# Gathered expert rows in a decoder layer: weighted rows in batches of two, tables asked for in turn

## The chip, the cores and the metric

The kernel runs on one core of a Trainium2 chip. The metric is the device time of one execution in microseconds (us); less is better.

## What is computed

One layer of a decoder over 1024 prompt tokens and 32 sample tokens (8 sequences of 4), width 1024, fp32: modulated RMSNorm, an input projection, a short gated convolution beside windowed attention, an output projection, and then a layer of 16384 single-neuron experts. This last part takes most of the time:

```
q = (x @ wq).reshape(tokens, 8 heads, 2, 128)
sc = einsum('thpc,hpnc->thpn', q, keys)            # 128 keys for each half
s_top, i_top = top_k(sc, 16)
best, pos = top_k(sum of all 16 x 16 pairs, 16)
experts = i_top[0] * 128 + i_top[1] at pos
act = gelu(einsum('thkd,td->thk', u_tab[experts], x))
y = einsum('thk,thkd->td', softmax(best) * act, v_tab[experts])
```

So each token needs, for 8 heads, 16 rows of `u_tab` and 16 of `v_tab`, each 1024 floats (4 KB). The outputs are the normed sums and the new key, value and convolution states.

## The kernel before, in words

**Units.** The tokens stand in 33 groups of 32. A unit is one group with four heads: 128 partitions (32 tokens x 4 heads), 16 experts each, so 66 units (`UNITS`). For a unit the kernel gathers 16 U rows and 16 V rows; one gather brings one row for each of 128 partitions, 128 x 4 KB, by an indirect DMA of GpSimd. Both tables have a ring of eight rows in SBUF, `Ur` and `Vr` (`RING` = 8).

**GpSimd** (`gather_u`, line 510, gather at 516; `gather_v`, gather at 527) asks for the rows in program order. U rows go in batches of two, each of which waits until DVE has done the dots of the batch four before (`dots_done`); batch 0 of a unit waits for its indices (`idx_ready`). V rows go in batches of four (`VB` = 4, four batches a unit, `NV`, over two ring halves), each of which waits until PE has weighed the batch two before (`pv_done`). The order is two U batches of unit n, one V batch of unit n-1, and so on. At the end, V rows of the last unit go to the U ring (`gather_last`, 536) and to the V ring (558).

**DVE** does the dots (`dots`, 1557: one instruction a row, 1024 products against the replicated token, summed), and between the batches of unit n the six parts of the top-16 selection of unit n+1 (`top`, 1505 to 1551; the last writes the indices `eid` at 1551, after the dots of batch 5), and pieces of earlier stages. **ACT** does gelu (1160), the softmax exponent (1123), and builds 16 diagonal blocks `dsel` of 128 x 32 that hold the weights (`selectors`, 1168).

**PE** sums the weighted rows: `weigh(m, q)` multiplies `dsel` (32 columns) with V rows 4q to 4q+3, first the four rows on columns 0 to 511 into bank 0, then on columns 512 to 1023 into bank 1; row k writes the 32 partitions `j = k % 4`. Each matmul shows as two instructions in the trace. Two units (the two halves of the heads) add up in the banks:

```
for half in range(2):
    for k in range(q * VB, (q + 1) * VB):
        j = k % 4
        last = mm(PS[j * GT:(j + 1) * GT, half, :], dsel[m % 2][:, k, :], rows[:, k % RING, half * 512:(half + 1) * 512], ...)
```

Then ACT copies both banks to `Yp` (`take_y`, 1178), and `combine` (862) sums the four blocks of 32 partitions through `sel` (four identity blocks below each other). `gated` and `normed` on DVE finish 128 tokens at a time.

**Order around it.** PE, ACT and DVE each run a loop over units n with four slots q. In a slot PE does the first piece of `gap(n, q)`, the combine (slot 1 of odd n), the other pieces, queries or scores for later tokens, and at its end `weigh(n-1, q)`. `replicate` (764), which puts the group's tokens where DVE reads them, stands ahead of slot 0 of even n. The pieces are what is left of the earlier stages, in a fixed list (`WOVEN`) dealt out by rules of load (`gaps`, at most 1, 3, 2 and 1 in slots 0 to 3): X transposes (660), Q and W query and score products (667, 676), I input projection (684), VN, KN, UT transposes (601, 603, 656), S, P, V of attention (618, 624, 629), H0, H1 output projection (696), T transposes (701). A piece on PE waits for the copy of the one before it by ACT or DVE; pieces go up to unit 20. Of its slots 17 hold more than one, for example:

| unit | slot 0 | slot 1 | slot 2 | slot 3 |
|---|---|---|---|---|
| 1 | T | X, X, X | X, X | Q |
| 3 | Q | Q | Q, W | W |
| 13 | I | I, VN, KN | UT, S | S |
| 14 | P | S, P, V | S, P | S |
| 18 | H1 | T, H0 | H1, T | H0 |

Of the kernel before, what the change touches and what calls it, by code (L numbers as in the profile page):

```python
# [7 lines left out]
D = 1024  # L8
# [27 lines left out]
VB = 4  # L36
# [88 lines left out]
def build(nc, a, out):  # L125
    ctx = ExitStack()
    with ctx:
# [80 lines left out]
        Yp, x2b, g2v, gfv = (R(38048 + D * i, D) for i in range(4))  # L208
# [238 lines left out]
        def _(po):  # L447
# [84 lines left out]
            def gather_last(q):  # L532

                po.wait_ge(s["dots_done"], (UNITS - 1) * NU + 6 + 2 * q)
                for k in range(q * VB, (q + 1) * VB):
                    po.indirect_dma_start(
                        out=Ur[:, k % RING, :], out_offset=None, in_=a["peer_v"],
                        in_offset=bass.IndirectOffsetOnAxis(ap=eid[(UNITS - 1) % 4][:, k:k + 1], axis=0),
                    ).then_inc(last_ld[q], 16)

            for n in range(UNITS - 1):
                for q in range(NV):
                    if n < UNITS:
                        gather_u(n, 2 * q)
                        gather_u(n, 2 * q + 1)
                    if n >= 1:
                        gather_v(n - 1, q)
            for q in range(NV):
                gather_u(UNITS - 1, 2 * q)
                gather_u(UNITS - 1, 2 * q + 1)  # L550
                if q == NV - 1:
                    gather_last(0)
                gather_v(UNITS - 2, q)
            gather_last(1)
            for q in (2, 3):
                po.wait_ge(s["pv_done"], (UNITS - 2) * NV + q + 1)
                for k in range(q * VB, (q + 1) * VB):
# [3 lines left out]
                    ).then_inc(v_ld[q % VBUFS], 16)  # L561
# [3 lines left out]
        def _(pe):  # L565
# [271 lines left out]
            def weigh(m, q):  # L837
                pe.wait_ge(s["diag_ready"], m + 1)
                rows = Vr
                if m < UNITS - 1:  # L840
                    pe.wait_ge(v_ld[q % VBUFS], 16 * VB * ((m * NV + q) // VBUFS + 1))
                elif q < 2:
                    pe.wait_ge(last_ld[q], 16 * VB)
                    rows = Ur
                else:
                    pe.wait_ge(v_ld[q % VBUFS], 16 * VB * (m * NV // VBUFS + 1))
                if q == 0 and m % 2 == 0 and m >= 2:
                    pe.wait_ge(s["y_ev"], m // 2)
                for half in range(2):
                    for k in range(q * VB, (q + 1) * VB):  # L850
                        j = k % 4
                        last = mm(PS[j * GT:(j + 1) * GT, half, :], dsel[m % 2][:, k, :], rows[:, k % RING, half * 512:(half + 1) * 512],  # L852
                                  start=m % 2 == 0 and q == 0, stop=m % 2 == 1 and q == NV - 1)
                last.then_inc(s["pv_done"], 1)

            def combine(g):
# [4 lines left out]
                for half in range(2):  # L861
                    last = mm(PS[p:p + GT, 2 + half, :], sel[:, :], Yp[:, half * 512:(half + 1) * 512], start=True, stop=True)  # L862
# [5 lines left out]
            for n in range(UNITS + 2):  # L868
# [3 lines left out]
                for q in range(NV):  # L872
# [8 lines left out]
                    if q == NV - 1 and FIRST <= n + 2 < UNITS:  # L881
                        scores(n + 2)
                    if q == NV - 1 and n == FIRST - 1 or q == 1 and n >= FIRST and t < TT:
                        queries(t, h)
                    if 1 <= n <= UNITS:
                        weigh(n - 1, q)
# [3 lines left out]
        def _(ac):  # L890
# [280 lines left out]
            def take_y(g):  # L1171
                ac.wait_ge(s["pv_done"], min(2 * g + 2, UNITS) * NV)
                if g:
                    ac.wait_ge(s["pe_cmb"], g)
                if g == 0:
                    ac.wait_ge(s["sc_st"], 16)
                for half in range(2):
                    last = act_(Yp[:, half * 512:(half + 1) * 512], PS[:, half, :], ACT.Copy)  # L1178
                last.then_inc(s["y_ev"], 1)

            for n in range(UNITS + 2):
# [8 lines left out]
                left = gap(n - 1, NV - 1)  # L1190
# [12 lines left out]
                for q in range(NV - 1):  # L1203
# [473 lines left out]
```

## Time and profile before

| | us |
|---|---|
| median of 3 timed executions | 3490.13 |
| lowest, highest | 3469.93, 3493.14 |
| profiled execution, span from first to last instruction | 3228.3 |

The profile shows one execution, and of its time only the span; start and end of the program lie around it. In its rows PE is TensorE, PEld its weight load, DVE VectorE, ACT ScalarE, POOL GpSimd, SP the sync engine; "L852" is a line of the kernel. The idle time before an instruction is put down to what ended it; "issue" means that no wait ended it. [...]

### The profile page before, as it was taken

To read this page: it belongs to the slowest core of one execution; us is meant where nothing else is said; L and a number is where in the kernel's file an instruction comes from. 1 tells how busy PE (TensorE), PEld (TensorE's weight loads), DVE (VectorE), ACT (ScalarE), POOL (GpSimd) and SP (SyncE) were. 2 spreads that over 40 slices of the span, in tenths; PEclk is the share of its full clock that TensorE was granted. 3 is DMA by queue.
4 is the path that set the end of the run, shared out by engine and by line. 5 is a ranking of instruction groups with operands and counts; after the bars stand their busy time and mean duration, and the time that the engine had idled before them with its cause. 6 is when DMAs were issued, how large, how long until landed. Compare 5 with 4: busy or idle time off the path is not lost.

```text
span 3228.3 us, 31544 instructions
## 1 busy us (share of the span) xinstructions
PE 1830.4 (57%) x9976; PEld 857.1 (27%) x9976; DVE 2038.7 (63%) x5142; ACT 705.5 (22%) x1970; POOL 2058.7 (64%) x2211
## 2 busy tenths in 40 slices
PE   5998757776746776374444444444444444454543
PEld 2456543333312222141111212211121112121200
DVE  3335736666668867566666766666666666666663
ACT  2122112212214322122222211122222222211211
POOL 1233647676656656577777777777777777777774
PEclk8999778888867787686676666677767767666567
DMA  9727999999999999999999999999999999999997
GB/s 325 262 96 247 366 395 385 410 410 410 410 342 367 378 372 409 406 409 410 409 407 405 402 411 405 407 402 410 402 407 404 406 406 405 403 408 402 406 408 298
DMA packets 393188, 1228.50 MB, mean 381 GB/s; under 512 B 54563, under 2 KB 104719, under 8 KB 389678
## 3 DMA queue, kind: packets, MB, share of 16 engines
q0 software_dynamic: 305728, 1109.92, 86.8%
q1 hardware_dynamic: 46314, 75.12, 6.6%
q10 hardware_dynamic: 40980, 41.44, 3.9%
q8 instruction: 79, 1.29, 0.2%
q14 instruction: 87, 0.71, 0.1%
HBM read 1211.31 MB, written 16.04 MB: 380 GB/s over the span
## 4 chain that ended last, share of the span: by engine, by line
POOL 30%; DMA 28%; DVE 15%; issue 12%; PE 11%; DVEq 2%; ACTq 1%; ACT 1%; SPq 1%; POOLq 0%
DMA arena<-in_peer_u,eid 22%; POOL arena L516 15%; POOL arena L527 14%; DVE arena L1557 9%; DMA arena<-in_peer_v,eid 4%; PE PS L722 3%; PE PS L852 2%; PE PS L696 1%; DVE arena L1546 1%; ACTq L956 1%; PE PS L684 1%; PE PS L667 1%; DVE ef L1549 1%; DVE arena L1541 1%; PE PS L580 1%
## 5 line engine op out<-in xcount | busy, mean ns | idle before, releaser
L1557 DVE CUSTOM_DVE_ANT_0 arena<-arena,PS 128x1024 f32<-128x1024 f32 x1056 | 1244.3, 1216 | 795.9 <-DMA arena<-in_peer_u,eid 606.7
L852 PE MATMUL PS<-arena 128*32 128x512 f32 x4224 | 829.8, 924 | 1162.5 <-DMA arena<-in_peer_v,eid 1145.4
L516 POOL DMA_INDIRECT arena<-in_peer_u,eid x1056 | 997.8, 945 | 491.7 <-issue 294.7
L527 POOL DMA_INDIRECT arena<-in_peer_v,eid x1040 | 982.8, 945 | 476.3 <-issue 290.5
L852 PEld LDWEIGHTS PS<-arena 128*32 128x32 f32 x4224 | 165.8, 144 | 1611.4 <-issue 1604.3
L1168 ACT ACTIVATE arena<-sel,wgt 128x32 f32<-128x32 f32 x1056 | 230.7, 310 | 21.5 <-DVE wgt L1568 21.0
L684 PE MATMUL PS<-arena 128*128 128x256 f32 (+1 forms) x576 | 176.9, 463 | 14.3 <-DVE arena L1400 14.3
L822 PEld LDWEIGHTS PS<-arena 128*128 128x128 f32 x1280 | 156.3, 203 | 48.0 <-issue 48.0
L822 PE MATMUL PS<-arena 128*128 128x128 f32 x1280 | 163.7, 289 | 0.0
L1156 ACT ACTIVATE arena<-PS 128x256 f32<-128x256 f32 x42 | 16.1, 384 | 661.3 <-PE PS L833 661.3
L1151 ACT ACTIVATE arena<-PS 128x256 f32<-128x256 f32 (+1 forms) x48 | 17.1, 357 | 612.6 <-PE PS L822 612.6
L684 PEld LDWEIGHTS PS<-arena 128*128 128x128 f32 x576 | 114.7, 205 | 99.7 <-issue 40.7
L722 PE MATMUL PS<-arena 128*128 128x416 f32 x288 | 115.4, 547 | 6.5 <-DMA arena<-in_w_in 4.6
L696 PE MATMUL PS<-arena 128*128 128x512 f32 (+1 forms) x192 | 88.8, 617 | 9.1 <-ACT arena L1051 9.1
L1557 DVE DVE_READ_ACCUMULATOR2_ANT act<- 128x1 f32 x1056 | 87.0, 82 | 0.0
L1160 ACT ACT_TABLE_LOAD x66 | 84.7, 1283 | 1.2
L1123 ACT ACT_TABLE_LOAD x62 | 79.5, 1283 | 2.7 <-ACT arena L1051 1.2
L862 PE MATMUL PS<-arena,sel 128*32 128x512 f32 x132 | 74.3, 691 | 1.2 <-ACT arena L1178 1.2
L1178 ACT ACTIVATE arena<-PS 128x512 f32<-128x512 f32 x66 | 35.8, 594 | 172.9 <-PE PS L852 172.9
L722 PEld LDWEIGHTS PS<-arena 128*128 128x128 f32 x288 | 54.9, 200 | 58.7 <-issue 52.5
L1568 DVE SCALAR_TENSOR_TENSOR wgt<-gex,grec,gel 128x16 f32<-128x16 f32 x66 | 15.6, 236 | 75.0 <-ACT gel L1160 74.4
L667 PEld LDWEIGHTS PS<-arena 128*128 128x128 f32 x512 | 59.1, 196 | 7.9 <-issue 6.5
(241 smaller groups left out, 1958.0 us busy)
## 6 DMA issues: line engine op xcount, KB each, us to landing
arena<-in_w_ada SPq DMA_DIRECT2D x24, 1024.0 KB, 8.3
arena<-in_peer_u,eid POOLq DMA_INDIRECT x1056
arena<-in_peer_v,eid POOLq DMA_INDIRECT x1056, 7.1
arena<-in_peer_wq ACTq DMA_DIRECT2D x10, 1024.0 KB, 5.6
arena<-in_peer_wq SPq DMA_DIRECT2D x4, 2048.0 KB, 37.9
arena<-in_w_in SPq DMA_DIRECT2D x14, 512.0 KB, 8.1
arena<-in_w_in ACTq DMA_DIRECT2D x14, 512.0 KB, 15.0
arena<-in_x_prompt ACTq DMA_DIRECT2D x8, 512.0 KB, 8.4
```

The costliest lines, as they stand in the source:

```text
L516: po.indirect_dma_start(out=Ur[:, k % RING, :], out_offset=None, in_=a["peer_u"], in_offset=bass.IndirectOffsetOnAxis(ap=eid[m % 4][:, k:k ...
L527: po.indirect_dma_start(out=Vr[:, k % RING, :], out_offset=None, in_=a["peer_v"], in_offset=bass.IndirectOffsetOnAxis(ap=eid[m % 4][:, k:k ...
L667: last = mm(PS[:, 6 + n % 2, half * 256 + (t - 1) * 128:half * 256 + t * 128], wqA[(PH - 3 + n) % 3][:, k, half * 128:(half + 1) * 128], ( ...
L684: last = mm(PS[:, 6 + half, 0:hi - lo], winB[pos % 3][:, k, :], hTB[:, k, lo:hi], start=k == 0, stop=k == KT - 1)
L696: last = mm(PS[0:r, 6 + half, :], zq[n][:, k, :], wout[:, k, half * 512:(half + 1) * 512], start=k == 0, stop=k == KT - 1)
L722: last = mm(PS[:, pos % 4, 0:NA], win[pos % 4][:, k, :], hT[:, k, :], start=k == 0, stop=k == KT - 1)
L822: last = mm(PS[:, 6, half * r:(half + 1) * r], wq[:, k, c * 128:(c + 1) * 128], rhs[:, k, :], start=k == 0, stop=k == KT - 1)
L852: last = mm(PS[j * GT:(j + 1) * GT, half, :], dsel[m % 2][:, k, :], rows[:, k % RING, half * 512:(half + 1) * 512], start=m % 2 == 0 and q ...
L1123: act_(gex[:, par, :], best[:, par, :], ACT.Exp, bias=nbest[:, par, :], accum_out=gsum[:, par:par + 1]).then_inc(s["exp_done"], 1)
L1160: act_(gel[:, m % 2, :], act[:, m % 2, :], ACT.Gelu).then_inc(s["gelu_done"], 1)
L1168: last = act_(dsel[par][:, k, :], sel[:, :], ACT.Copy, scale=wgt[:, par, k:k + 1])
L1557: last = ve.tensor_tensor_reduce(out=Ur[:, k % RING, :], in0=Ur[:, k % RING, :], in1=hP, scale=1.0, scalar=0.0, op0=ALU.mult, op1=ALU.add, ...
```

## The change

V rows go in batches of two as well: eight batches a unit over four ring parts. GpSimd asks for two U rows and two V rows in turn. `weigh` takes two rows on both column halves: row k, half h writes the 32 partitions `2h + k % 2` of one bank, and the bank changes with every pair of units, so that `take_y` is one instruction and may lag by one pair. `Yp` becomes two buffers of 512 columns, and `combine` contracts 64 partitions for each half. PE weighs the first batch of a slot behind the slot's first piece, ahead of the combine and the other pieces, and the second at the slot's end.

```diff
-VB = 4
+VB = 2
...
-        Yp, x2b, g2v, gfv = (R(38048 + D * i, D) for i in range(4))
+        Yp = [R(38048 + 512 * i, 512) for i in range(2)]
+        x2b, g2v, gfv = (R(39072 + D * i, D) for i in range(3))
...
             for n in range(UNITS - 1):
-                for q in range(NV):
-                    if n < UNITS:
-                        gather_u(n, 2 * q)
-                        gather_u(n, 2 * q + 1)
+                for b in range(NV):
+                    gather_u(n, b)
                     if n >= 1:
-                        gather_v(n - 1, q)
+                        gather_v(n - 1, b)
...
-            def weigh(m, q):
+            def weigh(m, b):
...
-                if q == 0 and m % 2 == 0 and m >= 2:
-                    pe.wait_ge(s["y_ev"], m // 2)
-                for half in range(2):
-                    for k in range(q * VB, (q + 1) * VB):
-                        j = k % 4
-                        last = mm(PS[j * GT:(j + 1) * GT, half, :], dsel[m % 2][:, k, :], rows[:, k % RING, half * 512:(half + 1) * 512],
-                                  start=m % 2 == 0 and q == 0, stop=m % 2 == 1 and q == NV - 1)
+                if b == 0 and m % 2 == 0 and m >= 4:
+                    pe.wait_ge(s["y_ev"], m // 2 - 1)
+                for k in range(b * VB, (b + 1) * VB):
+                    for half in range(2):
+                        j = 2 * half + k % 2
+                        last = mm(PS[j * GT:(j + 1) * GT, m // 2 % 2, :], dsel[m % 2][:, k, :], rows[:, k % RING, half * 512:(half + 1) * 512],
+                                  start=m % 2 == 0 and b == 0, stop=m % 2 == 1 and b == NV - 1)
...
-                    last = mm(PS[p:p + GT, 2 + half, :], sel[:, :], Yp[:, half * 512:(half + 1) * 512], start=True, stop=True)
+                    last = mm(PS[p:p + GT, 2 + half, :], sel[half * 64:half * 64 + 64, :], Yp[g % 2][half * 64:half * 64 + 64, :], start=True, stop=True)
...
-                for q in range(NV):
+                for q in range(4):
                     for i in gap(n, q)[:1]:
                         piece(i)
+                    if 1 <= n <= UNITS:
+                        weigh(n - 1, 2 * q)
                     if q == 1 and n % 2 == 1 and n >= 3:
                         combine((n - 3) // 2)
...
                     if 1 <= n <= UNITS:
-                        weigh(n - 1, q)
+                        weigh(n - 1, 2 * q + 1)
...
-                if g:
-                    ac.wait_ge(s["pe_cmb"], g)
+                if g >= 2:
+                    ac.wait_ge(s["pe_cmb"], g - 1)
...
-                for half in range(2):
-                    last = act_(Yp[:, half * 512:(half + 1) * 512], PS[:, half, :], ACT.Copy)
-                last.then_inc(s["y_ev"], 1)
+                act_(Yp[g % 2], PS[:, g % 2, :], ACT.Copy).then_inc(s["y_ev"], 1)
```

GpSimd where unit 1 ends and unit 2 begins, before (`eid` with a number is the unit's index buffer, u and v the tables):

```order
L527 DMA arena<-in_peer_v,eid0 128x1024 x4
L516 DMA arena<-in_peer_u,eid1 128x1024 x4
L527 DMA arena<-in_peer_v,eid0 128x1024 x4
L516 DMA arena<-in_peer_u,eid2 128x1024 x4
L527 DMA arena<-in_peer_v,eid1 128x1024 x4
```

and the same place in the changed kernel (line 517 is the U gather, 528 the V gather):

```order
L517 DMA arena<-in_peer_u,eid1 128x1024 x2
L528 DMA arena<-in_peer_v,eid0 128x1024 x2
L517 DMA arena<-in_peer_u,eid1 128x1024 x2
L528 DMA arena<-in_peer_v,eid0 128x1024 x2
L517 DMA arena<-in_peer_u,eid2 128x1024 x2
L528 DMA arena<-in_peer_v,eid1 128x1024 x2
```

Batch 5 of U is the first half of the four U rows in the second line of the first piece, and the first line of the second piece is batch 6.

PE in unit 14, from `replicate` on, before (852 weighs, 764 replicates, 624 is P, 618 S, 629 V of attention):

```order
L764 MATMUL PS<-ident,arena 128x128 x8
L624 MATMUL PS<-ident,arena 128x128 x8
L852 MATMUL PS<-arena 32x512 x8
L618 MATMUL PS<-arena 128x256 x4
L624 MATMUL PS<-ident,arena 128x128 x8
L629 MATMUL PS<-arena 64x512 x4
L852 MATMUL PS<-arena 32x512 x8
L618 MATMUL PS<-arena 128x256 x4
L624 MATMUL PS<-ident,arena 128x128 x8
L852 MATMUL PS<-arena 32x512 x8
```

and in the changed kernel (851 weighs, the pieces' lines are two less):

```order
L762 MATMUL PS<-ident,arena 128x128 x8
L622 MATMUL PS<-ident,arena 128x128 x8
L851 MATMUL PS<-arena 32x512 x8
L616 MATMUL PS<-arena 128x256 x4
L851 MATMUL PS<-arena 32x512 x4
L622 MATMUL PS<-ident,arena 128x128 x8
L627 MATMUL PS<-arena 64x512 x4
L851 MATMUL PS<-arena 32x512 x4
L616 MATMUL PS<-arena 128x256 x4
L851 MATMUL PS<-arena 32x512 x4
L622 MATMUL PS<-ident,arena 128x128 x8
L851 MATMUL PS<-arena 32x512 x4
```

In slots with one piece the two batches stay side by side (x8). In slots 1 and 2 the first stands between the S piece and the P piece.

## Rows read from the trace of the kernel before

**Rows 1.** The page's parts 1 and 2: busy times, DMA share and GB/s in 40 slices.
```profile
PE 1830.4 (57%) x9976; PEld 857.1 (27%) x9976; DVE 2038.7 (63%) x5142; ACT 705.5 (22%) x1970; POOL 2058.7 (64%) x2211
...
DMA  9727999999999999999999999999999999999997
GB/s 325 262 96 247 366 395 385 410 410 410 410 342 367 378 372 409 406 409 410 409 407 405 402 411 405 407 402 410 402 407 404 406 406 405 403 408 402 406 408 298
```

**Rows 2.** Windows of two stretches: time, busy times of engines, PEclk, DMA share, GB/s.
```profile
600.00:800.00 200.00, 140.13 (x592) 69.60 (x593) 130.69 (x329) 45.46 (x126) 134.88 (x141) 0.85 1.04 410
2000.00:2200.00 200.00, 92.78 (x560) 38.29 (x562) 133.88 (x347) 43.69 (x125) 144.76 (x155) 0.69 1.02 405
```

**Rows 3.** Waits of GpSimd, 1400 to 3100 us: total, times, longest.
```profile
POOL arena L516 <- DVE eid L1551: 81.4, 41, 2.8
POOL arena L527 <- PE PS L852: 20.1, 25, 2.8
```

**Rows 4.** Timeline 2007 to 2030 us: start, length, engine, line, [idle before <- releaser].
```profile
2007.10 1.22 DVE L1557 CUSTOM_DVE_ANT_0 arena<-arena,PS 128x1024 f32<-128x1024 f32 x1
...
2011.05 0.18 DVE L1551 SCALAR_TENSOR_TENSOR eid<-ef 128x16 int32<-128x16 f32 x1
...
2011.49 0.94 POOL L516 DMA_INDIRECT arena<-in_peer_u,eid  x1 [2.29 <-DVE eid L1551]
...
2012.73 0.94 POOL L516 DMA_INDIRECT arena<-in_peer_u,eid  x1 [0.30 <-issue]
...
2021.36 3.64 PE L852 MATMUL PS<-arena 128*32 128x512 f32 x16 [5.70 <-DMA arena<-in_peer_v,eid]
```

**Rows 5.** Windows of the seven stalls of the DMA queue, columns as in rows 2.
```profile
346.00:362.00 16.00, 9.04 (x44) 5.00 (x48) 13.78 (x38) 1.68 (x3) 5.87 (x7) 0.61 0.59 203
478.00:496.00 18.00, 11.76 (x232) 8.29 (x232) 8.62 (x28) 10.55 (x25) 7.23 (x8) 0.83 0.79 238
910.00:926.00 16.00, 10.04 (x53) 4.28 (x53) 14.66 (x31) 2.23 (x5) 5.81 (x7) 0.79 0.60 198
976.00:990.00 14.00, 10.58 (x57) 4.48 (x54) 11.79 (x23) 5.29 (x15) 7.36 (x8) 0.87 0.75 261
1022.00:1034.00 12.00, 8.00 (x44) 3.70 (x40) 10.12 (x20) 4.00 (x16) 7.45 (x8) 0.80 0.85 293
1066.00:1080.00 14.00, 10.80 (x56) 4.50 (x56) 11.20 (x22) 3.73 (x12) 6.09 (x6) 0.81 0.68 236
1170.00:1188.00 18.00, 15.38 (x55) 6.14 (x57) 4.16 (x5) 1.44 (x3) 7.50 (x8) 0.97 0.73 261
```

**Rows 6.** Timeline of PE and GpSimd in the stall at 980 us.
```profile
959.00 1.99 PE L618 MATMUL PS<-arena 64*128 64x256 f32 x8
...
968.89 1.97 PE L624 MATMUL PS<-ident,arena 128*128 128x128 f32 x8 [7.90 <-DVE arena L1417]
...
977.55 2.64 PE L852 MATMUL PS<-arena 128*32 128x512 f32 x16
...
980.51 0.94 POOL L527 DMA_INDIRECT arena<-in_peer_v,eid  x1 [11.00 <-PE PS L852]
```

**Rows 7.** First request after the stall at 915 us, and the queue two us later.
```profile
918.36 0.95 POOL L527 DMA_INDIRECT arena<-in_peer_v,eid  x1 [12.81 <-PE PS L852]
...
920.00:922.00 2.00, 2.00 (x12) 1.35 (x15) 2.00 (x5) 0.00 (x0) 1.49 (x2) 1.00 0.91 245
```

**Rows 8.** Waits of DVE, 940 to 1100 us: the first.
```profile
DVE arena L1557 <- DMA arena<-in_peer_u,eid: 20.2, 6, 15.2
```

**Rows 9.** Timeline of PE in the stall at 480 us.
```profile
481.30 3.32 PE L676 MATMUL PS<-arena 128*32 128x128 f32 x64 [26.78 <-ACT arena L1033]
```

**Rows 10.** The chain that ended last, at the end.
```profile
3213.07 1.96 PE PS L852 x16
3215.05 1.09 ACT arena L1178 x2
3216.19 1.92 PE PS L862 x4
```

More of the change, by code:

```diff
@@ L534, in gather_last @@
                 po.wait_ge(s["dots_done"], (UNITS - 1) * NU + 6 + 2 * q)
-                for k in range(q * VB, (q + 1) * VB):
+                for k in range(q * RING // 2, (q + 1) * RING // 2):
                     po.indirect_dma_start(
@@ L541, in _ @@
             for n in range(UNITS - 1):
-                for q in range(NV):
-                    if n < UNITS:
-                        gather_u(n, 2 * q)
-                        gather_u(n, 2 * q + 1)
+                for b in range(NV):
+                    gather_u(n, b)
                     if n >= 1:
-                        gather_v(n - 1, q)
-            for q in range(NV):
-                gather_u(UNITS - 1, 2 * q)
-                gather_u(UNITS - 1, 2 * q + 1)
-                if q == NV - 1:
+                        gather_v(n - 1, b)
+            for b in range(NV):
+                gather_u(UNITS - 1, b)
+                if b == NV - 1:
                     gather_last(0)
-                gather_v(UNITS - 2, q)
+                gather_v(UNITS - 2, b)
             gather_last(1)
-            for q in (2, 3):
-                po.wait_ge(s["pv_done"], (UNITS - 2) * NV + q + 1)
-                for k in range(q * VB, (q + 1) * VB):
+            for b in range(NV // 2, NV):
+                po.wait_ge(s["pv_done"], (UNITS - 2) * NV + b + 1)
+                for k in range(b * VB, (b + 1) * VB):
                     po.indirect_dma_start(
@@ L560, in _ @@
                         in_offset=bass.IndirectOffsetOnAxis(ap=eid[(UNITS - 1) % 4][:, k:k + 1], axis=0),
-                    ).then_inc(v_ld[q % VBUFS], 16)
+                    ).then_inc(v_ld[b % VBUFS], 16)
         @block.tensor
@@ L880, in _ @@
                         queries(AHEAD, HU * (n - FIRST + 2) + q)
-                    if q == NV - 1 and FIRST <= n + 2 < UNITS:
+                    if q == 3 and FIRST <= n + 2 < UNITS:
                         scores(n + 2)
-                    if q == NV - 1 and n == FIRST - 1 or q == 1 and n >= FIRST and t < TT:
+                    if q == 3 and n == FIRST - 1 or q == 1 and n >= FIRST and t < TT:
                         queries(t, h)
                     if 1 <= n <= UNITS:
-                        weigh(n - 1, q)
+                        weigh(n - 1, 2 * q + 1)
         @block.scalar
@@ L1189, in _ @@
                     gelu(n - 1)
-                left = gap(n - 1, NV - 1)
+                left = gap(n - 1, 3)
                 after_weight = [i for i in left if PIECES[i][0] in ("S", "H1", "KN", "VN", "UT")]
@@ L1202, in _ @@
                     piece(i)
-                for q in range(NV - 1):
+                for q in range(3):
                     for i in gap(n, q):
```

11 lines of the change are left out of this document (5 added, 6 removed).

## The prediction

> **What bounds the kernel now.** I read the page's busy shares and slices first, then windows by stage, then what GpSimd waits for, then the timeline at one place in the even stretch and at one stall. No compute engine is full: POOL 64%, DVE 63%, PE 57% of the span, but the DMA line stands at 9 in every slice from the fifth of 40 on, most of them at 402 to 411 GB/s [rows 1]. What moves there are the gathered rows: 2112 gathers of 128 x 4 KB, 512 KiB each. From 600 to 800 us the queue runs at share 1.04 and 410 GB/s, from 2000 to 2200 us at 1.02 and 405 GB/s [rows 2]. 524,288 bytes at 405 GB/s is 1.29 us a gather ("row" below), or 41.4 us for the 32 rows of a unit. GpSimd needs 0.94 + 0.30 = 1.24 us to ask for one [rows 4], 39.7 us a unit, so it gets ahead until a wait holds it back.
>
> What holds it in the even stretch, 1400 to 3100 us, is mostly the indices of the next unit: 81.4 us in 41 waits, against 20.1 us in 25 for weighed V rows [rows 3]. These waits cost nothing while rows are still queued. At 2007.10 DVE starts the dots of batch 5 of a unit, at 2011.05 it writes the next indices, at 2011.49 GpSimd asks again, and the V rows asked for before that moment are weighed only at 2021.36, when they have landed [rows 4]. So some 9.9 us of queued transfers covered the gap.
>
> The queue does run dry in seven short stalls, all before 1200 us [rows 5]. Length times (1 - share) gives the idle time: 16 x 0.41 = 6.6, 18 x 0.21 = 3.8, 16 x 0.40 = 6.4, 14 x 0.25 = 3.5, 12 x 0.15 = 1.8, 14 x 0.32 = 4.5, 18 x 0.27 = 4.9: 31.5 us. By bytes, against 410 GB/s, it is 16 x 0.505 + 18 x 0.420 + 16 x 0.517 + 14 x 0.363 + 12 x 0.285 + 14 x 0.424 + 18 x 0.363 = 44.9 us. That is all that a better ordered queue can win there. The stall at 980 shows their make: PE does an S piece at 959.00, waits 7.90 us for DVE before the P piece at 968.89, and reaches the weigh only at 977.55; GpSimd sat 11.00 us on V rows that this weigh frees and asked again at 980.51 [rows 6].
>
> **The change, part by part.** Bytes, gathers, matmuls of weigh (4224) and their shapes stay. What changes is where the weighs stand and how many rows one wait covers.
>
> *The even stretch: 0.* In bytes it has no idle time to win. What the alternation costs is cover: after batch 5 of U the queue used to hold four V, four U and four V rows (12) before the next unit's first U row; now v5, u6, v6, u7, v7 are 10. That is 10 x 1.29 = 12.9 us in place of 15.5. From the start of the dots to the new request is 4.39 us [rows 4]; after a dry queue the first request went out at 918.36 and the queue was back at share 0.91 in 920 to 922 [rows 7], so add 2 to 4 us. 12.9 - 4.4 - 4 = 4.5 us are left at worst: still covered. PE has slack there too. In an odd unit the second batch of slot 1 now comes behind a first batch (half of 3.64 us), the combine and a query piece, and may be 3 us late; the next request that needs it is 14 rows, 18 us, behind.
>
> *The stalls.* Count what GpSimd may have asked for beyond the last weighed slot of four. Before, with PE held up anywhere in slot q, it stops at the V rows of q+2: 20 rows. Now, if PE is held ahead of the slot's first batch, it stops at batch 2q+4: 18 rows. If it is held between the two, at 2q+5: 22 rows. The first batch stands behind the first piece of a slot only, so a slot with more pieces is of the second kind. Two rows are 2.6 us. Besides, a release needs half a weigh: 3.64 us at the low clock level [rows 4], 1.96 at the high one [rows 10], so it comes 1.0 to 1.8 us sooner; I take 1.3. A stall of the second kind gains 3.9 us at most, one of the first loses 1.3.
>
> - 346 (X pieces), 910 (I, combine, VN, KN) and 1170 (T, H0) are of the second kind: 3 x 3.9 = 11.7 us.
> - 976, 1022 and 1066 too, by their S, P and V pieces: min(3.5, 3.9) + min(1.8, 3.9) + 3.9 = 9.2 us of queue time. But from 944 on DVE scarcely waits: of its 20.2 us of waits for U rows from 940 to 1100 us the longest, 15.2, is the tail of the 910 stall [rows 8]. Only 5.0 us are left there, and a queue that is ahead of a full DVE wins no more than that. Between 0 and 5.0 I take 3.
> - 478 is of the first kind: PE waits 26.78 us for ACT's copy in a slot with one piece (W) [rows 9]. +1.3 us.
>
> Together -13.4 us, between 0 (the piece chain, not the queue, sets the pace between the stalls) and -44.9.
>
> *Waits of PE moved forward.* Pieces behind the first batch of a slot now wait for V rows to land. In the stall of rows 6 those rows had two further batches of time before DVE's answer came, so nothing. Seventeen slots have more than one piece; without that cover each could pay up to a batch pair, 5.2 us, 88 us in all. PE waits for DVE in such slots as it is, so I take 0 and keep two of them, 10 us, for the upper end.
>
> *take_y and combine* are off the path except at the end. There the chain runs 1.96 us of weigh, 1.09 us of ACT, 1.92 us of combine [rows 10]. The last batch is half: -1.0. One ACT instruction for two: -0.5. Combine does as many matmuls with 64 rows contracted in place of 128; a 128 x 512 pass here costs by its columns, so 0, or half (-1.0) if the two halves run beside each other; I take -0.5. Sum -2.0. [...]
>
> *Sum.* -13.4 - 2.0 = -15.4 us on the profiled span of 3228.3, to 3212.9. The profiled execution shows only its span; the timed median is 3490.13, 261.8 us longer (start and end of the program, where nothing is changed). 3490.1 - 15.4 = 3474.7 us, -0.4%.
>
> **Rivals.**
> *The shorter cover runs dry (slower).* Mechanism: DVE writes a unit's indices so late that the ten rows behind batch 5 have all landed. It decides from a delay of 12.9 us between that batch's landing and the first bytes of the next unit; now it is 7 to 8.4. For: the index wait is already the commonest in the even stretch [rows 3]. Against: 9.9 us in hand today [rows 4], of which 2.6 go. One dry us in each of 64 units gives 3474.7 + 64 = 3539 us.
> *The whole idle time comes back (faster).* If each stall is only just too long, finer release ends all: -44.9 - 2.0 = 3443 us. For: all seven end in a wait for weighed V rows. Against: [rows 8], and 4 to 6 us of a single stall are more than two rows cover.
> *Nothing moves.* DVE and the piece chain, not the queue, set the pace from 300 to 1200 us; a queue that is ahead only meets the next stall earlier. Then the end alone is left: 3488 us. For: DVE's few waits [rows 8] and the 7.90 us that PE waits for DVE [rows 6].
>
> **How the numbers follow.** Forecast (3475) 0.50, nothing moves 0.22, all idle back 0.22, cover dry 0.06. About 1%, 35 us, is what a measurement of this kernel can tell from no change: the three runs shown lie 23 us apart. Within it fall the forecast (but for 0.02 of its better edge) and the case in which nothing moves: 0.48 + 0.22 = 0.70. Over 1% faster are the case of 3443 and that edge: 0.24. Slower: 0.06. The range: from 3440 (all idle time back, with a little room for the spread) to 3508 (nothing gained, the 10 us of PE's moved waits, and half the runs' spread).
>
> **What would show it.** Right: windows from 1400 to 3100 us still at 405 GB/s, share 1.02, with GpSimd's wait for indices grown, since it gets there with fewer rows out; the dips near 350, 915 and 1175 us 3 to 5 us shorter; the dip near 480 not shorter; DVE's waits for U rows from 944 to 1100 close to none; the last weigh at 1.0 us and one ACT copy of 0.6. Wrong: a DMA share under 1 in each unit right after the indices (cover dry); an unchanged sum over the seven dips (piece chain); PE sitting on V rows in front of P or H pieces with DVE waiting for those pieces; or new dips where there are none now.

## The result, and the profile after

| | changed | before, beside it |
|---|---|---|
| median, us | 3507.46 (7 executions) | 3484.1 (7) |
| lowest, highest | 3496.76, 3518.4 | 3469.93, 3493.14 |
| ratio, 95% interval | 1.0072 [1.0052, 1.0093] | |

The forecast was 3475.0 us, so the sign is wrong: 0.7% slower. That the time still lies in the stated range (3440 to 3508) is luck: the room at its upper end stood for PE's moved waits and the spread of the runs. The page of the changed kernel, parts 1 and 2 (the DMA line is the mean busy share of the 16 DMA engines; further down PEclk is the granted TensorE clock as a part of full speed):

```profile
PE 1920.7 (55%) x9976; PEld 867.1 (25%) x9976; DVE 2032.2 (58%) x5142; ACT 689.1 (20%) x1937; POOL 2058.9 (59%) x2211
...
DMA  9738999999998999999989999999999998999998
GB/s 328 234 104 297 365 333 396 398 383 385 369 382 304 390 400 405 360 347 381 374 336 362 373 357 359 361 367 353 350 364 352 363 344 337 359 346 358 366 368 310
```

Against [rows 1] DVE, ACT and GpSimd are busy for nearly the same time and PE for 90 us more, but the span is 3504.8 us, and from 1400 to 3100 us the slices stand at 336 to 381 GB/s instead of 402 to 411. The windows of the first stall of [rows 5] and of the second stretch of [rows 2]:

```profile
346.00:362.00 16.00, 8.97 (x39) 4.49 (x37) 13.01 (x38) 1.09 (x3) 7.67 (x9) 0.55 0.93 353
...
2000.00:2200.00 200.00, 81.92 (x473) 32.12 (x472) 111.24 (x293) 37.12 (x103) 128.41 (x137) 0.65 0.96 364
```

The dip at 350 us is gone as forecast (share 0.59 before). But 2000 to 2200 us, where nothing was to change, has fallen from share 1.02 to 0.96. One stretch of DVE in its timeline (columns as in rows 4), and the same stretch as a window:

```profile
2422.49 0.23 DVE L1567 SCALAR_TENSOR_TENSOR wgt<-gex,grec,gel 128x16 f32<-128x16 f32 x1 [3.15 <-ACT gel L1161]
2438.47 1.22 DVE L1556 CUSTOM_DVE_ANT_0 arena<-arena,PS 128x1024 f32<-128x1024 f32 x1 [15.74 <-remote]
```

```profile
2424.00:2438.00 14.00, 6.02 (x26) 0.66 (x24) 0.00 (x0) 2.33 (x11) 8.43 (x9) 0.50 1.03 413
```

DVE stands still for 15.74 us. "remote" means that the profile finds no instruction of this core whose end released the wait; what it stands for here is told below. GpSimd goes on asking meanwhile and the queue is at 413 GB/s. The trace of before has nothing like it. From this pair of traces alone one would call this the price of the change. So the first experiment was the kernel before once more.

### The profile page after: what moved, and what is told of

Same layout as the page of the kernel before. It is cut to its first block, busy times and chain, and to the rows that moved or that the text cites. A ratio compares the mean times of both kernels' runs of the same rounds, so it can differ in the third digit from the quotient of the medians.

```text
span 3504.8 us, 31774 instructions
## 1 busy us (share of the span) xinstructions
PE 1920.7 (55%) x9976; PEld 867.1 (25%) x9976; DVE 2032.2 (58%) x5142; ACT 689.1 (20%) x1937; POOL 2058.9 (59%) x2211
## 4 chain that ended last, share of the span: by engine, by line
another core or an unknown queue 28%; PE 19%; POOL 14%; issue 13%; DVE 9%; DMA 8%; ACT 6%; DVEq 2%; SPq 1%; ACTq 1%; POOLq 0%
POOL arena L528 7%; POOL arena L517 7%; PE PS L851 5%; DVE arena L1556 5%; DMA arena<-in_peer_v,eid 4%; DMA arena<-in_peer_u,eid 3%; PE PS L820 3%; PE PS L720 2%; PE PS L665 2%; ACT arena L1169 2%; PE PS L682 2%; PE PS L694 1%; PE PS L732 1%; PE PS L771 1%
## 5 line engine op out<-in xcount | busy, mean ns | idle before, releaser
L851 PE MATMUL PS<-arena 128*32 128x512 f32 x4224 | 882.9, 863 | 1174.3 <-DMA arena<-in_peer_v,eid 564.4
L851 PEld LDWEIGHTS PS<-arena 128*32 128x32 f32 x4224 | 139.6, 131 | 1715.2 <-issue 1313.8
L682 PE MATMUL PS<-arena 128*128 128x256 f32 (+1 forms) x576 | 188.3, 486 | 83.1 <-ACT arena L1042 33.9
L820 PE MATMUL PS<-arena 128*128 128x128 f32 x1280 | 187.7, 310 | 38.8 <-issue 33.8
L820 PEld LDWEIGHTS PS<-arena 128*128 128x128 f32 x1280 | 177.1, 222 | 92.2 <-issue 84.5
L682 PEld LDWEIGHTS PS<-arena 128*128 128x128 f32 x576 | 120.8, 215 | 167.0 <-issue 44.1
L1157 ACT ACTIVATE arena<-PS 128x256 f32<-128x256 f32 x42 | 16.1, 383 | 702.6 <-remote 613.2
L665 PE MATMUL PS<-arena 128*128 128x128 f32 x512 | 63.7, 280 | 10.7 <-issue 9.0
L720 PEld LDWEIGHTS PS<-arena 128*128 128x128 f32 x288 | 54.2, 198 | 57.7 <-issue 51.4
L665 PEld LDWEIGHTS PS<-arena 128*128 128x128 f32 x512 | 59.8, 194 | 20.3 <-issue 16.1
L762 PE MATMUL PS<-ident,arena 128*128 128x128 f32 x264 | 54.2, 367 | 9.7 <-issue 6.8
```

The lines of the kernel that those rows point to most:

```text
L665: last = mm(PS[:, 6 + n % 2, half * 256 + (t - 1) * 128:half * 256 + t * 128], wqA[(PH - 3 + n) % 3][:, k, half * 128:(half + 1) * 128], ( ...
L682: last = mm(PS[:, 6 + half, 0:hi - lo], winB[pos % 3][:, k, :], hTB[:, k, lo:hi], start=k == 0, stop=k == KT - 1)
L720: last = mm(PS[:, pos % 4, 0:NA], win[pos % 4][:, k, :], hT[:, k, :], start=k == 0, stop=k == KT - 1)
L820: last = mm(PS[:, 6, half * r:(half + 1) * r], wq[:, k, c * 128:(c + 1) * 128], rhs[:, k, :], start=k == 0, stop=k == KT - 1)
L851: last = mm(PS[j * GT:(j + 1) * GT, m // 2 % 2, :], dsel[m % 2][:, k, :], rows[:, k % RING, half * 512:(half + 1) * 512], start=m % 2 == 0 ...
```

## The experiments

**The kernel before, unchanged**

```diff
(no line changed)
```

> The kernel before, unchanged, for a second profile of it. Known so far: the profile shown of before spans 3228 us, but its timed runs take 3470 to 3493 us, and in the changed kernel span and time agree (3504.8 and 3507). Theory D (the profiled execution of before was a lucky one: in the timed ones the DMA queue and the engines run as unevenly as in the profile of the changed kernel): this profile spans some 3470 to 3490 us, the gathers run at 360 to 375 GB/s in the even stretch, with engines that stand still for up to 20 us for nothing that the profile shows. Rival L (3228 is how before always runs and some 260 us lie outside its span): span 3228 again, 405 GB/s. Ratio to before 0.998 to 1.002 either way.

Measured: 3481.56 us against 3482.96, ratio 0.9997 [0.9971, 1.0023]. Its trace spans 3476.2 us, not 3228.3. Its windows (2000 to 2200 us, then a standstill of DVE), and 10 us windows around another:

```profile
2000.00:2200.00 200.00, 85.63 (x488) 34.61 (x484) 120.45 (x318) 38.08 (x116) 130.69 (x139) 0.66 0.97 370
...
2136.00:2150.00 14.00, 8.00 (x40) 2.79 (x40) 0.00 (x0) 2.30 (x11) 8.76 (x11) 0.62 1.03 414
...
2220.00:2230.00 10.00, 2.25 (x32) 0.84 (x24) 2.92 (x8) 6.00 (x18) 7.55 (x9) 0.84 0.75 249
2230.00:2240.00 10.00, 4.67 (x24) 1.54 (x24) 0.00 (x0) 1.07 (x6) 7.44 (x8) 0.67 1.02 412
2240.00:2250.00 10.00, 7.46 (x47) 4.46 (x48) 1.88 (x3) 0.00 (x0) 3.75 (x4) 0.79 0.97 388
2250.00:2260.00 10.00, 2.20 (x19) 0.58 (x17) 9.34 (x32) 0.38 (x1) 6.21 (x7) 0.89 0.62 199
```

The same kernel has standstills too. From 2230 to 2240 us DVE does nothing while the queue runs at 412 GB/s; from 2240 to 2250 GpSimd, out of free ring slots, is busy for only 3.75 of 10 us; from 2250 on the queue has run dry, at 199 GB/s. DVE started again at 2248.12 us, so a standstill is paid from its end on, once the ring is full.

All runs fell under one of two conditions of the machine: in one, "even", the kernel before takes 3229 us (its medians lie between 3229.1 and 3229.8), as in the trace shown ahead of the prediction; in the other, "uneven", 3475 to 3484 us. It changed between sets of runs. Chip 15 showed both, so the chip alone does not decide it; but chips 0 and 5 showed only the even one, and no uneven set is on record from another chip than 15. Each kernel is compared with the kernel before, run beside it on the same chip.

**The parts of the change taken back one by one, uneven.** GpSimd's order (two U, two V batches, so four and four rows), everything else changed:

```diff
-                for b in range(NV):
+                for b in range(0, NV, 2):
                     gather_u(n, b)
+                    gather_u(n, b + 1)
                     if n >= 1:
                         gather_v(n - 1, b)
+                        gather_v(n - 1, b + 1)
...
```

> The changed kernel, but GpSimd asks for four U rows and four V rows in turn again (batches of two, PE's places as changed). Theory O (the alternation is what costs: two rows less of cover behind the unit's indices, and V rows block U rows sooner, so the queue runs dry more often under uneven engines): the ratio falls from 1.007 to 0.998 to 1.001. Theory P (PE's earlier wait for V rows ahead of pieces and queries costs): it stays at 1.006 to 1.009. Theory B (smaller batches themselves: twice as many waits and 230 instructions more): it stays at 1.005 to 1.009.

Measured: 1.0069 [1.0038, 1.0100]. PE's place (both weighs at the slot's end):

```diff
-                    if 1 <= n <= UNITS:
-                        weigh(n - 1, 2 * q)
...
                     if 1 <= n <= UNITS:
+                        weigh(n - 1, 2 * q)
                         weigh(n - 1, 2 * q + 1)
```

> The changed kernel, but both batches of a slot are weighed at the slot's end, as before (order of GpSimd and batches of two as changed). Theory P: the ratio falls to 0.998 to 1.001. Theories O and B: 1.005 to 1.009.

Measured: 1.0097 [1.0067, 1.0127]. Both edits together, which leaves the batches of two and the bank layout:

> The changed kernel with the order of GpSimd and the places of weigh on PE both as before: batches of two, one bank, one copy of y and the 64-row combine are left. Theory B: 1.005 to 1.009. Theories O and P: 0.996 to 1.001.

Measured: 1.0069 [1.0038, 1.0100]. What follows: order and place aren't what costs here; with both as before, the loss is still there, within the intervals.

**The layout alone, and waits alone, even.** The layout, one copy and the 64-row combine with batches of four, order and place as before:

```diff
-VB = 2
+VB = 4
...
-                                  start=m % 2 == 0 and b == 0, stop=m % 2 == 1 and b == NV - 1)
+                                  start=m % 2 == 0 and b == 0 and k < 2, stop=m % 2 == 1 and k >= TOPK - 2)
...
-                        weigh(n - 1, 2 * q + 1)
+                        weigh(n - 1, q)
```

> The changed kernel with VB = 4: batches of four, the order of GpSimd and the places of weigh on PE as before. Only the new layout is left: row by row on both halves, one bank that alternates, one copy of y, the 64-row combine. e4_both stood at 1.0069 with this layout and batches of two. Theory S (size: the batches of two cost): 0.997 to 1.001. Theory Y (the layout costs: four matmuls into one bank, or the combine's other tiling): 1.005 to 1.009.

Measured: 0.9995 [0.9986, 1.0004]; repeated twice:

> e5_layout again (new layout, batches of four): 0.9995 in the second condition. If this call meets the first: theory S (the size of the batches costs there, not the layout): 0.998 to 1.002. Theory Y (the layout costs there): 1.005 to 1.009. In the second condition 0.9995 again, within 0.001.

> e5_layout (new layout, batches of four) for the machine's first condition (before at some 3480 us), if this call meets it. Theory S (the size of the batches costs there): 0.998 to 1.002. Theory Y (the layout costs there): 1.005 to 1.009. In the second condition (before at some 3229 us): 0.9995 again.

0.9995 [0.9986, 1.0004] and 0.9990 [0.9981, 0.9999]. So 0 to -3 us of the 3229. The kernel before with one satisfied wait more for each half of a weigh:

```diff
                 for half in range(2):
+                    pe.wait_ge(s["diag_ready"], m + 1)
                     for k in range(q * VB, (q + 1) * VB):
```

> The kernel before with a second, already satisfied wait for diag_ready ahead of each half of each weigh: up to 528 instructions more on PE, nothing else. Theory I (the batches of two cost by their instructions: each engine's program is itself fetched over the full DMA queue, and the changed kernel has 230 instructions more): at least the loss of the change, 1.005 to 1.015. Rival (the price is in the waits' meaning, or in the layout): 0.998 to 1.002.

Measured: 1.0001 [0.9992, 1.0010]. (The page of before has two DMA queues of the kind "instruction": 1.29 and 0.71 MB, 0.2% and 0.1% of the 16 engines' span.) And again:

> The kernel before with one wait more on TensorE for each half of a weigh, already satisfied when it is reached, up to 528 in all. Where engines stand still: theory A, what loses there goes with the number of instructions and waits that the engines take in: 1.002 to 1.008. Theory B, it goes with who waits for what: 0.998 to 1.002. Where the machine runs evenly: 1.000 again.

0.9997 [0.9988, 1.0006]. A satisfied wait costs nothing in the even condition; the uneven one, for which the second was meant, was gone again.

**Batches of two, but PE waits for both batches of a slot at once** (order and place as before):

```diff
...
+                if b % 2 == 0 and (m < UNITS - 1 or b >= NV // 2):
+                    pe.wait_ge(v_ld[(b + 1) % VBUFS], 16 * VB * (...))
...
```

> e4_both, but PE waits for both batches of a slot to land before it weighs the first, then does all eight matmuls on end, as before; rows are still released to GpSimd by twos. Theory F (PE starts and stops on smaller pieces, with a start-up and a lower clock for each): the ratio falls from 1.007 to under 1.003. Theories Y and I: it stays at 1.005 to 1.009.

> e7_joint again (batches of two, GpSimd's order and PE's places as before, PE waits for both batches of a slot): 0.9976 in the second condition. If this call meets the first: theory F (the joint wait is what helps): under 1.003. Theory C (the condition decides, not the wait): 1.004 to 1.009 as e4_both. In the second condition 0.9976 again, within 0.001.

> e7_joint (batches of two, PE waits for both of a slot) for the first condition. Theory F (PE's starts on two rows cost): under 1.003. If batches of two cost for another reason, or the layout does: 1.005 to 1.009, as e4_both. In the second condition: 0.9975 again.

> As the version with batches of two, order and place as before, but TensorE waits for both batches of a slot at once, so that it weighs four rows in one stretch as before and only the release to GpSimd and the table's waits are by two. Where engines stand still (the kernel before at 3460 to 3500 us), the version with a wait for each batch stood at 1.0088 and the layout alone at 1.0027. Theory A, TensorE's stop between the two batches of a slot is the loss: 1.001 to 1.005, near the layout alone. Theory B, GpSimd's requests and releases by two are the loss: 1.006 to 1.011. Where the machine runs evenly: 0.9974 a fourth time.

All four runs were even: 0.9976 [0.9967, 0.9985], 0.9974 [0.9964, 0.9985], 0.9973 [0.9963, 0.9983], 0.9970 [0.9959, 0.9981], or -8 us. Of it 0 to 3 us are the layout's, which is in this version too; the finer release alone pays the other 5 to 8.

**The changed kernel again: even**

> The changed kernel again. So far the runs fall into two conditions of the machine: in one the kernel before takes 3458 to 3508 us and the engines stand still for 10 to 20 us at a time with nothing recorded that they wait for, in the other it takes 3225 to 3234 us and they don't. The change was timed in the first alone (1.0072). If this call meets the second: theory T (the stalls of the profile shown are shortened as the prediction has it, and what the change loses it loses only beside the standstills): 0.993 to 0.998. Rival U (the change costs in either condition): 1.003 to 1.009. If it meets the first: 1.005 to 1.009.

Measured: 3218.34 us against 3229.12, ratio 0.9963 [0.9949, 0.9977]. The change that lost 23 us wins 10.8 us (medians; 5 executions of it) in the condition of the trace that I had read. Windows over long stretches of it (columns as in rows 2):

```profile
270.00:400.00 130.00, 95.07 (x669) 64.49 (x668) 99.75 (x266) 29.82 (x72) 73.56 (x78) 0.88 0.91 337
400.00:600.00 200.00, 131.17 (x965) 79.25 (x963) 109.89 (x287) 41.70 (x107) 121.82 (x130) 0.85 1.01 393
900.00:1200.00 300.00, 193.20 (x790) 80.14 (x790) 231.15 (x550) 89.82 (x266) 182.35 (x188) 0.76 0.99 374
200.00:1400.00 1200.00, 800.52 (x4170) 417.53 (x4169) 783.83 (x1967) 280.63 (x768) 719.12 (x767) 0.81 0.97 373
1400.00:3100.00 1700.00, 870.56 (x4900) 342.00 (x4902) 1133.94 (x2921) 340.17 (x989) 1223.35 (x1300) 0.61 1.02 406
```

and of before (the trace shown ahead of the prediction):

```profile
270.00:400.00 130.00, 97.27 (x665) 65.12 (x664) 101.81 (x267) 29.84 (x72) 76.06 (x80) 0.84 0.89 334
400.00:600.00 200.00, 131.13 (x944) 79.53 (x942) 108.22 (x284) 41.84 (x109) 120.58 (x128) 0.85 1.02 394
900.00:1200.00 300.00, 187.39 (x759) 79.09 (x760) 225.46 (x529) 86.85 (x252) 171.84 (x180) 0.74 0.95 361
200.00:1400.00 1200.00, 802.24 (x4169) 422.05 (x4168) 778.36 (x1954) 286.24 (x780) 712.86 (x760) 0.81 0.96 370
1400.00:3100.00 1700.00, 822.19 (x4864) 346.54 (x4868) 1126.13 (x2923) 349.12 (x1003) 1221.98 (x1300) 0.68 1.02 406
```

The last column tells it: nothing from 1400 us on (406 and 406), and 373 against 370 GB/s ahead of it. 1200 x 3 / 373 = 9.7 us, nearly the whole gain, and 300 x 13 / 374 = 10.4 of it (-0.5 and +1.2 elsewhere) lie between 900 and 1200 us. The rates are whole GB/s, which leaves 1 to 3 us of doubt in each product, but the times at which DVE writes a unit's indices say the same: against before the changed kernel is 1.9 us late at unit 0 (272 us), 2.9 late at unit 12 (825 us), 6.6 early at unit 26 (1506 us) and 7.4 early at unit 65 (3139 us).

**Order and place, even**

> e2_order (changed kernel with the four-and-four order of GpSimd, PE's places as changed). In the first condition 1.007 as before. In the second condition, where the whole change is 0.9963: if half the gain is the alternation (fewer rows held back by one wait), 0.998; if the gain is PE's earlier first batch, 0.9965.

> e3_place (changed kernel with both batches of a slot at its end). In the first condition 1.009 as before. In the second condition: if the gain is PE's earlier first batch, which the prediction's stalls of the second kind rest on, 0.998 to 0.999; if it is the alternation or the smaller release, 0.9965.

Measured: without the alternation 3212.97 us, 0.9952 [0.9939, 0.9966], the best version of all; without the early place 3236.12 us, 1.0022 [1.0012, 1.0033], slower than before. Two of the seven stalls (columns as in rows 2) in the version without the early place:

```profile
346.00:362.00 16.00, 8.85 (x44) 4.98 (x48) 13.78 (x36) 1.68 (x3) 7.11 (x8) 0.61 0.70 241
...
910.00:926.00 16.00, 9.81 (x57) 4.32 (x58) 14.31 (x31) 1.73 (x3) 6.57 (x7) 0.79 0.57 188
```

and without the alternation, with two windows more:

```profile
346.00:362.00 16.00, 7.98 (x44) 4.52 (x48) 13.78 (x36) 1.68 (x3) 5.36 (x6) 0.71 0.81 287
...
910.00:926.00 16.00, 11.79 (x66) 4.85 (x67) 14.11 (x31) 4.36 (x13) 8.46 (x10) 0.82 0.84 250
...
1170.00:1188.00 18.00, 15.24 (x65) 5.77 (x64) 15.80 (x32) 8.40 (x18) 11.58 (x12) 1.00 1.01 386
...
1164.00:1168.00 4.00, 4.00 (x13) 1.82 (x10) 0.00 (x0) 0.00 (x0) 2.79 (x3) 1.00 0.74 263
```

The last two rows are a warning: in the window of [rows 5] the stall at 1170 us seems gone, but it has only moved out of it, to 1164 us, since this kernel is some 11 us ahead there. So the idle time is taken here from slices of 4 us over wider stretches (340 to 376, 470 to 502, 904 to 940, 960 to 1000, 1008 to 1040, 1050 to 1090 and 1156 to 1196 us), as length times (1 - share) of each slice below 1. Beside it stands how much later than before a profiled execution writes the indices of unit 26:

| version, even | seven stalls, us | indices of unit 26, us | time against before, us |
|---|---|---|---|
| before | 31.6 | 0 | 0 |
| layout alone | 31.2 | -2.8 | 0 to -3 |
| without the early place | 33.0 | +6.3 | +7 |
| joint wait, order and place as before | 23.4 | -9.3 | -8 |
| changed kernel | 16.1 | -6.6 | -10.8 |
| without the alternation | 16.0 | -16.0 | -16.5 |

The idle time tells which versions gain, but not how much: the last two have the same. (The profiled execution of the changed kernel took 3222.94 us, 4.6 above its median.)

With the alternation the early place is worth 3236.12 - 3218.34 = 18 us; the alternation costs 3218.34 - 3212.97 = 5 us. (These compare two sets of runs whose kernels before agree within 0.4 us.)

**Layout against batches, uneven.** The condition came back for two runs:

> The changed kernel with GpSimd's order (four U, four V rows) and PE's place of the weighs (both batches at a slot's end, each with a wait of its own) as before; batches of two and the new bank layout are left. Where the machine runs evenly (the kernel before at 3225 to 3235 us, 405 GB/s): the joint version with one wait for both batches stood at 0.9974, the layout alone at 0.9995. Theory A, finer release of V rows gives something where PE stands still: 0.993 to 0.997. Theory B, the batches in themselves are nothing and only the joint wait and the layout gave the 8 us: 0.9965 to 0.9995. Where engines stand still (the kernel before at 3460 to 3500 us): 1.005 to 1.009 again, as the same edits gave 1.0069 there.

> The kernel before with the new bank layout, copy and combine alone (batches of four, order and place as before). Where the machine runs evenly: 0.9985 to 1.0000, as three times already. Where engines stand still: theory A, the layout (four matmuls side by side on columns of both halves in one bank) is what loses there: 1.005 to 1.009. Theory B, the batches of two, with twice the waits and half the rows for each, lose there: 0.998 to 1.002.

Measured: batches of two with the layout 3508.24 us, 1.0088 [1.0055, 1.0121]; the layout alone 3488.28 us, 1.0027 [1.0001, 1.0052]; before 3474.7. Of 34 us between the medians, 14 come with the layout and 20 with the batches of two; by the ratios it is 31 us, of which 9 and 21. The two intervals do not overlap, so the batches of two do cost something here. The layout's share is barely told from nothing, and the same edits gave 1.0069 in the earlier set, so the split is rough. What GpSimd waits for from 1400 to 3100 us (columns as in rows 3), in the kernel before of the first experiment:

```profile
POOL arena L527 <- remote: 196.4, 78, 4.6
...
POOL arena L527 <- PE PS L852: 46.7, 8, 11.7
POOL arena L516 <- DVE act L1557: 37.2, 22, 6.3
```

and with batches of two and the layout:

```profile
POOL arena L528 <- remote: 160.0, 53, 4.9
...
POOL arena L517 <- DVE act L1559: 109.0, 57, 6.3
POOL arena L528 <- PE PS L855: 25.4, 18, 11.1
```

The waits move from V rows to U rows (DVE's dots): 37.2 us in 22 waits became 109.0 in 57. In sum they are nearly equal (280.3 and 294.4 us), so this names the place, and does not explain 20 us. In the chain that ended last the share of "another core or an unknown queue" rises as well, from 19% (before) and 21% (layout) to 30%.

**What the standstills wait for.** This kernel runs on one core, and the waits marked "remote" can be named from its code. GpSimd's at L527 is for weighed rows (`pv_done`). ACT's long ones (L1151, L1156 and L1178 of the kernel before) are for queries, scores and weighed sums. DVE's, at the first dots of every second unit, is for the replicated token (`rep_done`) and for landed U rows. All but the last are signals of TensorE. One such start of DVE in the trace shown ahead of the prediction (unit 38), then one in that of the first experiment (unit 40):

```profile
2026.94 1.22 DVE L1557 CUSTOM_DVE_ANT_0 arena<-arena,PS 128x1024 f32<-128x1024 f32 x1 [7.24 <-PE PS L764]
```

```profile
2233.91 1.09 PE L764 MATMUL PS<-ident,arena 128*128 128x128 f32 x8
...
2248.12 1.22 DVE L1557 CUSTOM_DVE_ANT_0 arena<-arena,PS 128x1024 f32<-128x1024 f32 x1 [20.65 <-remote]
```

In the first the semaphore event of `rep_done` stands 0.01 us after the end of the last transpose and DVE starts 0.04 us after that end. In the second the transposes end at 2235.01, the event stands at 2248.10 and DVE starts at 2248.12. The U rows, asked for from 2224.98 us on, are unlikely to be what it waited for: V rows asked for after them, from 2229.95 on, were being weighed at 2240.64. From the end of the transposes to the first dots the median over these units is 0.04 us in every even trace but that without the alternation (1.2 us). In the uneven ones it is 7.5 us before, 6.9 with the layout alone and 11.4 to 12.5 in the five traces with batches of two. So in the uneven condition TensorE's signals come late, and later with batches of two. Three things stay open. Ends of matmuls are modelled in the profile, so either the signal or the matmul itself may be late. How some 4 us more in each second unit become the loss of a version is not shown. And the uneven traces lack more than half of the semaphore events (16485 of 37727 DMA landings are recorded in that of the first experiment), so the recording was disturbed as well; whether it disturbs the kernel, or both have one cause, no run shows. The joint wait and the extra waits, meant to tell what about the batches costs, met the even condition.

## Why the prediction was wrong, step by step

**The step that failed** is in the sum: "the timed median is 3490.13, 261.8 us longer (start and end of the program, where nothing is changed)". Nothing of that size lies around the span. The execution profiled in the first experiment took 3478.1 us with a span of 3476.2; that of the changed kernel, even, 3222.94 with 3220.0. So 2 to 3 us lie around it. The trace shown and the times shown came from two conditions: the first had no standstills, the second spent 250 us on them. I applied a gain read in one to a time taken in the other, where every version with batches of two measured there loses 0.7 to 1.0%. Set beside the first experiment, in its own condition, the changed kernel runs at the same 357 GB/s from 200 to 1400 us, so the stalls gave nothing where -13.4 us was forecast, and at 357 instead of 364 GB/s from 1400 to 3100 us, 1700 x 7 / 364 = 33 us, where 0 was forecast; the spans differ by 28.6. (The other versions with batches of two split their loss otherwise, 346 to 355 GB/s in the first stretch and 361 to 365 in the second, so one trace of each does not fix the place.) A gap of 8% between span and time deserved to be a rival of its own; there was none.

Why batches of two lose there stays open; late signals of TensorE are what the traces show. Read against the condition of the trace, each step can be judged:

- **Even stretch, 0: right.** 406 GB/s before and after. GpSimd gets to the index wait with fewer rows out, so waits longer, as forecast: 89.9 us instead of 81.4. Its waits in the changed kernel, even:

```profile
POOL arena L517 <- DVE eid L1550: 89.9, 41, 4.1
POOL arena L517 <- DVE act L1556: 22.5, 68, 2.1
POOL arena L528 <- PE PS L851: 4.8, 13, 0.8
```

  The rival in which the shorter cover runs dry is out in this condition: no loss in the stretch. (By its own terms, 4.4 us and 2 to 4 more, its delay is 6.4 to 8.4 us and not 7 to 8.4; nothing hangs on it.) The waits for weighed V rows fell from 20.1 us to 4.8.

- **Stalls, -13.4: right in kind, somewhat too large.** Over 200 to 1400 us it was -9.7. The stalls themselves, in the changed kernel, even:

```profile
346.00:362.00 16.00, 6.37 (x35) 3.18 (x35) 13.56 (x41) 1.68 (x3) 6.31 (x8) 0.71 0.95 354
478.00:496.00 18.00, 13.47 (x240) 8.95 (x240) 9.69 (x28) 10.78 (x25) 8.55 (x10) 0.83 0.78 248
910.00:926.00 16.00, 9.75 (x53) 4.03 (x53) 14.66 (x32) 2.00 (x4) 8.57 (x10) 0.79 0.90 307
976.00:990.00 14.00, 10.48 (x56) 4.60 (x56) 12.57 (x26) 6.03 (x17) 10.37 (x11) 0.88 1.02 393
1022.00:1034.00 12.00, 8.91 (x36) 2.88 (x36) 10.12 (x21) 5.93 (x19) 8.30 (x9) 0.52 0.87 301
1066.00:1080.00 14.00, 10.40 (x56) 4.33 (x56) 12.35 (x24) 4.43 (x14) 8.12 (x9) 0.88 0.75 238
1170.00:1188.00 18.00, 15.24 (x53) 6.39 (x52) 11.09 (x20) 6.63 (x11) 11.40 (x12) 1.00 0.85 285
```

  At 346, 910 and 1170 the idle time went from 6.6, 6.4 and 4.9 to 0.8, 1.6 and 2.7 us: -12.8 in these windows (-11.5 in the wider stretches above), where 3 x 3.9 = 11.7 was forecast. But 270 to 400 us as a whole gained only 1.2 us, and the indices of unit 3 (400 us) are written 3.6 us later than before (those of unit 0: 1.9 later), so that what 346 gave was given back beside it. That is the "queue that is ahead only meets the next stall earlier" of the third rival, and the oversized term: 3.9 us there should have been 0 to 1. At 976, 1022 and 1066 it is 9.8 to 5.1, -4.7 where I took -3. At 478, of the first kind, 3.8 to 4.0, where +1.3 was said: the right sign at most. The stalls at 976 to 1066 us gave more than forecast and that at 346 less, so part of the agreement in the sum is luck.

- **DVE's waits between 940 and 1100 us**, which were to shrink from 20.2 us to close to none, are 7.5 (row below). So they shrank by 12.7 us and not to none; 900 to 1200 us gained 10.4 us where the forecast's terms give 3.9 + 3 + 3.9 = 10.8.

```profile
DVE arena L1556 <- DMA arena<-in_peer_u,eid: 7.5, 3, 4.3
```

- **The count of 18, 20 and 22 rows: the times fit it, the idle times only in part.** In the version without the early place PE is always held ahead of both batches, so each stall is of the first kind: 7 x 1.3 = 9.1 us lost by the forecast's numbers, against +7 measured, though the idle time grew by only 1.4 us. With the joint wait the order is as before, so 20 rows as before and each release 1.3 us sooner: 9.1 us won, against 8 measured, of which up to 3 are the layout's. The alternation without the early place loses; the early place outweighs it. But the count says that the two orders differ only in stalls of the first kind; taking the alternation back also changed those of the second: the one at 1170 shrank from 3.3 to 1.4 us of idle time, the one at 346 grew from 1.4 to 3.6. That is not explained.

- **Waits of PE moved forward, 0: not contradicted.** The version without the alternation has the early place and wins most.

- **The end, -2.0: right once the clock is the same.** Last steps of the chain in the changed kernel, even:

```profile
3205.26 1.97 PE PS L851 x8
3207.26 0.61 ACT arena L1178
3207.91 1.94 PE PS L861 x4
```

  The granted clock is 0.50 here (window 3205 to 3209 us), where it was 1.00 in [rows 10] (3212 to 3216 us; the 3.64 us of [rows 4] were at 0.50, 2021 to 2025 us), so 8 instructions of weigh take what 16 took, and only ACT's 0.48 us shows. The version without the alternation ends at the high level (window of its last weigh, then of its combine):

```profile
3197.00:3199.00 2.00, 1.06 (x8) 0.19 (x8) 0.00 (x0) 0.48 (x1) 0.00 (x0) 1.00 0.00 0
3199.00:3201.00 2.00, 1.05 (x4) 0.14 (x4) 0.73 (x1) 0.12 (x1) 0.00 (x0) 1.00 0.00 0
```

  Weigh 1.96 to 1.06, ACT 1.09 to 0.61, combine 1.92 to about 1.05: -0.9 - 0.5 - 0.9 = -2.3 us. The 64-row combine takes about half of the time of the 128-row one, the better end of the bound of 0 to -1.0, as if its halves ran beside each other. That a pass costs by its columns fits the trace shown: 288 instructions of L684 with 256 columns took 73.4 us, 288 with 384 took 103.6, or 0.25 and 0.36 us each, and with 64 rows contracted and 256 columns it was 0.27 us (L618, 112 in 30.7).

The other two rivals are out as well: with the whole idle time back the changed kernel would stand at -47 us, with nothing moved at -2; it stands at -10.8 in the even condition and at +23 in the uneven one.

## What to carry to other kernels

Compare the span of the trace with the times before anything is read from it; here they lay 2 to 3 us apart whenever they were of one execution, and a gap of 260 us meant that the trace was of another condition, so the same kernel should have been profiled again. Fixed windows mislead once a change shifts the schedule: follow the stall, or an event of each unit. Of a finer release of buffers: by itself it paid 5 to 8 us here, with half of the work put ahead of what holds the releasing engine 16.5 us, and turning the order of the requests as well took 5 us back. A change of a few tenths of a per cent can have one sign in one condition of the machine and the other in the next (here 0.9963 and 1.0072), so both want measuring.

## What the runs showed of the hardware

- One core's program ran under two conditions, 7.6 to 7.9% apart (3229 and 3475 to 3484 us). In the uneven one DVE stood still 15 times in 1700 us, 221.2 us in all, the longest 21.5, at the start of every second unit, for a signal of TensorE: from the end of the transposes it belongs to, to the first dots, it was 7.5 us (median), and 0.04 us in the even one:

```profile
DVE arena L1557 <- remote: 221.2, 15, 21.5
```

- It isn't a constant cap on the memory: the 10 us windows of the first experiment reach 412 GB/s and fall to 199 two windows later. From 1400 to 3100 us the mean is 364 GB/s there and 406 in the even condition. Why the two conditions differ no run here shows.

- Where the queue set the pace the granted clock didn't: from 1400 to 3100 us it was 0.61 in the changed kernel, even, and 0.68 before, PE's busy time 870.56 against 822.19 us, and the queue at 406 GB/s in both.
